# Seven feed-forward stages: one 2x2 pair of blocks of the down projection as seven products, with two of its weight sums made by adding transfers

## What is computed

```python
def swiglu(x, w_gate, w_up, w_down):
    return (jax.nn.silu(x @ w_gate) * (x @ w_up)) @ w_down

# first stack, per layer
x = x + 0.5 * swiglu(rmsnorm(x, ffn1_norm[l]), ...)
x = x + hybrid_mixer(rmsnorm(x, mix_norm[l]), ...)
x = x + 0.5 * swiglu(rmsnorm(x, ffn2_norm[l]), ...)
```

## Time and profile before

| | us |
|---|---|
| median of 3 runs (2436.86 to 2438.19) | 2436.91 |
| the profiled execution | 2436.97 |
| its span (first to last instruction) | 2435.2 |
| PE busy | 2407.2 (99%) |
| DVE busy | 1710.7 (70%) |
| ACT busy | 1255.4 (52%) |

### The profile page before, as it was taken

How to read it: one execution, slowest core, us unless ns; L and a number is a source line. 1 busy time by engine, 2 the same in 40 slices (tenths; PEclk the granted TensorE clock), 3 DMA queues, 4 the chain that set the end, 5 groups by cost and what they waited for, 6 DMA issues and landing times.

```text
span 2435.2 us, 30841 instructions
## 1 busy us (share of the span) xinstructions
PE 2407.2 (99%) x12606; PEld 2053.7 (84%) x12606; DVE 1710.7 (70%) x1755; ACT 1255.4 (52%) x1367; POOL 205.5 (8%) x358
## 2 busy tenths in 40 slices
PE   8999999999999999999999999999999999999998
PEld 6889998888889988888889878888888898778887
DVE  6555867857866778768658657777687677577884
ACT  5435545535537545445435664555455356645552
POOL 0100200101100100100100010001001000100010
PEclk9999999999999999999999999999999999999999
DMA  8765445856754446856864445468568544454672
GB/s 333 238 216 191 157 154 209 276 202 214 275 202 182 162 158 225 277 203 226 272 215 175 163 151 212 169 224 280 201 211 276 186 182 156 151 197 170 220 272 105
DMA packets 82549, 504.42 MB, mean 207 GB/s; under 512 B 11609, under 2 KB 12761, under 8 KB 30185
## 3 DMA queue, kind: packets, MB, share of 16 engines
q1 hardware_dynamic: 61488, 433.23, 49.4%
q0 software_dynamic: 19744, 67.65, 8.7%
q10 hardware_dynamic: 1176, 1.58, 0.4%
HBM read 476.72 MB, written 25.69 MB: 206 GB/s over the span
## 4 chain that ended last, share of the span: by engine, by line
PE 91%; DVE 5%; ACT 3%; issue 1%; DMA 1%; SPq 0%; POOL 0%; DVEq 0%; POOLq 0%; ACTq 0%
PE acc L709 23%; PE acc L711 22%; PE acc L710 22%; PE acc L677 4%; PE acc L678 4%; PE acc L679 4%; DVE w_lo L576 2%; PE aux L810 1%; PE aux L812 1%; PE aux L811 1%; PE aux L944 1%; ACT w_hi L568 1%; DMA raw<-in_w 1%; ACT tmp L1689 1%; PE bc L810 1%
## 5 line engine op out<-in xcount | busy, mean ns | idle before, releaser
L576 DVE TENSOR_TENSOR w_lo<-raw,w_hi 128x2048 fp32r<-128x2048 f32 (+1 forms) x438 | 978.7, 2245 | 489.1 <-ACT w_hi L568 487.9
L568 ACT ACTIVATE w_hi<-raw 128x2048 fp32r<-128x2048 f32 (+1 forms) x438 | 822.2, 1882 | 551.7 <-PE acc L711 387.6
L709 PE MATMUL acc<-w_hi,x_hi 128*128 128x512 f32 (+1 forms) x1624 | 633.4, 390 | 3.6 <-DVE x_lo L1941 2.1
L711 PE MATMUL acc<-w_lo,x_hi 128*128 128x512 f32 (+1 forms) x1624 | 628.5, 387 | 0.0
L710 PE MATMUL acc<-w_hi,x_lo 128*128 128x512 f32 (+1 forms) x1624 | 628.4, 387 | 0.0
L709 PEld LDWEIGHTS acc<-w_hi,x_hi 128*128 128x128 f32 x1624 | 305.0, 188 | 69.4 <-issue 6.1
L711 PEld LDWEIGHTS acc<-w_lo,x_hi 128*128 128x128 f32 x1624 | 305.0, 188 | 62.9
L710 PEld LDWEIGHTS acc<-w_hi,x_lo 128*128 128x128 f32 x1624 | 305.1, 188 | 61.7 <-issue 1.0
L709 PE MATMUL acc<-w_hi,h_parts 128*128 128x512 f32 x704 | 274.5, 390 | 0.0
L711 PE MATMUL acc<-w_lo,h_parts 128*128 128x512 f32 x704 | 274.0, 389 | 0.0
L710 PE MATMUL acc<-w_hi,h_parts 128*128 128x512 f32 x704 | 273.9, 389 | 0.0
(11 more groups left out here) (435 smaller groups left out, 2729.0 us busy)
## 6 DMA issues: line engine op xcount, KB each, us to landing
raw<-in_w SPq DMA_DIRECT2D x399, 1024.0 KB, 4.9
squares<-tmp POOLq DMA_DIRECT2D x40, 512.0 KB, 3.3
tmp<-squares POOLq DMA_DIRECT2D x160, 128.0 KB, 4.4
raw<-in_w SPq DMA_DIRECT2D x18, 512.0 KB, 4.8
tmp<-in_norm_gb POOLq DMA_DIRECT2D x8, 1024.0 KB, 5.9
tmp<-in_norm_gb POOLq DMA_DIRECT2D x6, 512.0 KB, 3.7
tmp<-in_gate_rows POOLq DMA_DIRECT2D x12, 256.0 KB, 2.9
squares<-tmp POOLq DMA_DIRECT2D x8, 256.0 KB, 2.8
```

The source lines that it names most:

```text
L568: nc.scalar.activation(w_hi[:, slot, 0:kind], raw[:, slots[c], 0:kind], ACT.Copy).then_inc(hi_done, 1)
L576: nc.vector.tensor_tensor(w_lo[:, slot, 0:kind], raw[:, slots[c], 0:kind], w_hi[:, slot, 0:kind].bitcast(F32), ALU.subtract).then_inc(lo_d ...
L709: nc.tensor.matmul(out, vh, wh, start=first and k == 0, stop=False)
L711: last = nc.tensor.matmul(out, vh, wl, start=False, stop=last_k and k == nk - 1)
```

## The change

In the seven FFNs behind the first, the down stage has 15 places instead of 12. The blocks of K 0 to 1023 (hid(0) and hid(1)) by both halves of the columns and both token tiles were eight block products; they are now seven, strewn among the plain chunks. The order of the places, with d = chunk 25 of the FFN and the matmuls of each:

d+0 plain, hid(2) (24); d+1 T1 (12); d+2 plain, hid(3) (24); d+3 B11 (12); d+4 B22 (12); d+5 plain, hid(4) (24); d+6 T2 (12); d+7 half, hid(5) (12); d+8 T3 (12); d+9 half, hid(5) (12); d+10 B21 (12); d+11, d+12, d+13 plain for token tile 0 (12 each); then d+11, d+12 for token tile 1 (24), d+14 T4 (12), `x_turn`, and d+13 for token tile 1 (12).

- T1 = B12 + B11: SP loads B12, and POOL then issues a transfer that adds B11 to it in `raw` (`grow`). T2 = T1 + B22 and T3 = T2 - B11 are made by DVE in `raw`. T4 = T2 + B21 is again an adding transfer, behind the last `permute`.
- The sums of hidden activations (`h_sums`, four adds of 128x512 on DVE) are made in the up stage behind `hid_low(1)`, into tmp 28 to 35 (`HQ4`); that is where the norm's gains go. They are split into `x_hi`, `x_lo` (`hsum_high`, `hsum_low`) once the up stage has used these.
- Three shared products stand in PSUM banks `bc` and `aux` and are added to `x` by six DVE instructions (`x_add`). B22, B21 and T4 go into the normal tiles.
- POOL: `load_norm` has moved from ahead of the six `permute`s to ahead of the last, behind a wait for `sum_parts` (the fourth `hsum_low`), since it overwrites the sums. The third `permute` waits for `h_sums`, and `grow` for T1 follows it.
- `add_out` of columns 0 to 511, token tile 1, has moved from the down stage into `norm`.
- A few semaphores are merged.

```diff
+DOWN = (2, D12, 3, D11, D22, 4, None, 0, None, 1, D21, 8, 9, 10, None)
+D_FIRST, D_T1, D_THREE, D_B11, D_B22, D_FOUR, D_T2, D_HALF0, D_T3, D_HALF1, D_B21, D_TWO, D_LAST2, D_LAST, D_T4 = range(15)
+DOWN_SLOT_OF = {D_FOUR: 3, D_T2: 5, D_HALF0: 3, D_T3: 5, D_B21: 3, D_TWO: 3, D_LAST2: 3, D_LAST: 3, D_T4: 8}
+DOWN_ADD = {D_T1: D11, D_T4: D21}
...
@@ PE @@
+                    plain(d + D_FIRST, 0, 8, 4, True, False)
+                    pe.wait_ge(sum_parts, 8 * b + 5)
+                    pe.wait_ge(outs_ready, 3 * b + 1)
+                    product(d + D_T1, e_, *s1, True)
+                    plain(d + D_THREE, 0, 12, 4, False, False)
+                    pe.wait_ge(kept_silu, 2 * b + 2)
+                    product(d + D_B11, b_, *h11, True)
+                    pe.wait_ge(sum_parts, 8 * b + 7)
+                    bank_free(tile + 2)
+                    into(d + D_B22, tile + 2, *s4, True, False)
+                    plain(d + D_FOUR, 0, 16, 4, False, False)
+                    pe.wait_ge(x_added, 6 * b + 3)
+                    product(d + D_T2, b_, *s2, False)
+                    plain(d + D_HALF0, 0, 20, 2, False, False)
+                    pe.wait_ge(sum_parts, 8 * b + 8)
+                    pe.wait_ge(x_added, 6 * b + 4)
+                    product(d + D_T3, b_, *s3, False)
...
+                    into(d + D_T4, tile + 1, *h22, False, True, 0)
+                    if parts(s + 1):
+                        x_turn(s + 1, 0)
+                    plain(d + D_LAST, 1, 16, 4, False, True, (1,), 2)
...
@@ ACT @@
+                    ahead.to(d + 2)
+                    hid_high(3)
+                    ended_chunk(act, d - 1)
+                    hsum_high(0)
+                    silu(5, 0)
+                    silu(5, 1)
+                    hsum_high(1)
+                    hsum_high(2)
+                    ahead.to(d + 3)
+                    hsum_high(3)
+                    choose_sqrt()
+                    ahead.to(d + 4)
+                    hid_high(4)
+                    ahead.to(d + 7)
+                    hid_high(5)
...
@@ DVE, norm @@
-                if not early:
+                if not early or s:
                     add_out(s, 0, 1)
                 add_out(s, 1, 1)
...
@@ POOL @@
+            def grow(c):
+                at = c - DOWN_AT - base[s]
+                if at == D_T1:
+                    pool.wait_ge(loaded[slots[c]], 16 * landings[c])
+                else:
+                    pool.wait_ge(lo_done, c - D_T4 + D_T2 + 1)
+                    pool.wait_ge(weight_sum, sums.index(c - D_T4 + D_T3) + 1)
+                pool.dma_start(raw[:, slots[c], 0:WIDE], t[f"w{WIDE}"][more[c]], accum_op=ALU.add).then_inc(weight_added, 16)
...
-                    load_norm(s + 1)
+                    if s == 0:
+                        load_norm(s + 1)
...
                     for i in range(6):
+                        if s and i == 2:
+                            pool.wait_ge(sum_ready, 8 * f)
+                        if s and i == 5:
+                            pool.wait_ge(sum_parts, 8 * f)
+                            load_norm(s + 1)
                         permute(f, i)
+                        if s and i == 2:
+                            grow(base[s] + DOWN_AT + D_T1)
+                    if s:
+                        grow(base[s] + DOWN_AT + D_T4)
```

More of the change, by code:

```diff
@@ L69, in transfers, with packed @@
                 place[kind] += 12
+            elif sub == "ffn" and j == DOWN_AT:
+                n = len(DOWN)
+                def packed(at):
+                    return place[WIDE] + at - (at > 5)
+                for q, at in DOWN_ADD.items():
+                    more[len(out) + q] = packed(at)
+                for q, at in enumerate(DOWN):
+                    if q in (D_HALF0, D_HALF1):
+                        out.append(place[HALF] + at)
+                    else:
+                        out.append(None if at is None else packed(at))
+                place[WIDE] += 10
+                place[HALF] += 2
             else:
@@ L73, in transfers @@
             j += n
-    return out
+    return out, more
 def wide(w):
@@ L260, in __init__ @@
                     self.block(c + last)
-                for last in (c + 24, c + 30, c + 36):
-                    self.block(last)
+                self.block(c + 24)
+                self.chunks(c + DOWN_AT + D_B21, c + DOWN_AT + D_B21 + 1)
+                self.chunks(c + DOWN_AT + D_T4, c + DOWN_AT + D_T4 + 1)
+                self.block(c + DOWN_AT + D_T4)
             if kind == "mix1":
@@ L313, in program @@
     ends = Ends(base).at
-    places = transfers()
+    places, more = transfers()
     group_at = [base[s] + GROUP_AT for s in range(n_subs) if subs[s] == "ffn"]
+    down_at = [base[s] + DOWN_AT for s in range(n_subs) if subs[s] == "ffn"]
     slots, landings, on_slot = [], [], [0] * RING
     for c, place in enumerate(places):
-        within = next((c - g for g in group_at if 0 <= c - g < len(GROUP)), 0)
-        slots.append(slots[c - SLOT_OF.get(within, RING)] if c >= RING else c)
+        back = next((SLOT_OF.get(c - g, RING) for g in group_at if 0 <= c - g < len(GROUP)), RING)
+        back = next((DOWN_SLOT_OF.get(c - d, RING) for d in down_at if 0 <= c - d < len(DOWN)), back)
+        slots.append(slots[c - back] if c >= RING else c)
         on_slot[slots[c]] += place is not None
         landings.append(on_slot[slots[c]])
-    sums = [g + q for g in group_at for q in (G_T1, G_T2, G_T3, G_T4)]
+    sums = [c for g, d in zip(group_at, down_at)
+            for c in (g + G_T1, g + G_T2, g + G_T3, g + G_T4, d + D_T2, d + D_T3)]
+    grown = sorted(more)
     with ExitStack() as ctx:
@@ L1450, in ups, with hsum_high @@
                         ahead.to(c0 + 4 * i + 7)
+                def hsum_high(q):
+                    act.wait_ge(sum_ready, 8 * (f - 1) + 4 + q + 1)
+                    nc.scalar.activation(HSUM_HI[q], HQ4[q].rearrange("p k a j -> p k (a j)"), ACT.Copy).then_inc(sum_hi, 1)
                 def group(g, b):
@@ new lines, in hsum_low, with x_add @@
+                def hsum_low(q):
+                    dve.wait_ge(sum_hi, 8 * (f - 1) + 4 + q + 1)
+                    V_.tensor_tensor(HSUM_LO[q], HQ4[q].rearrange("p k a j -> p k (a j)"), HSUM_HI[q].bitcast(F32),
+                                     ALU.subtract).then_inc(sum_parts, 1)
+                def x_add(c, bank, n, tt, sign):
+                    xs = x[:, tt, 512 * n:512 * n + 512]
+                    ended_chunk(dve, c)
+                    V_.scalar_tensor_tensor(xs, bank, sign * weight_of(s), xs, ALU.mult, ALU.add).then_inc(x_added, 1)
@@ new lines, in down @@
+                def down(d, b):
+                    b_, e_ = aux[:, 1, :], bc[:, :]
+                    ahead.to(d + 2)
+                    hid_low(3)
+                    hsum_low(0)
+                    ahead.to(d + 3)
+                    times(5, 0)
+                    times(5, 1)
+                    turn_squares(5)
+                    ahead.to(d + 4)
+                    dve.wait_ge(lo_done, d + D_T1 + 1)
+                    V_.tensor_tensor(weights(d + D_T2), weights(d + D_T1), weights(d + D_B22), ALU.add).then_inc(weight_sum, 1)
+                    hid_low(4)
+                    hsum_low(1)
+                    hsum_low(2)
+                    ahead.to(d + 5)
+                    x_add(d + D_T1, e_, 1, 0, 1.0)
+                    x_add(d + D_T1, e_, 1, 1, 1.0)
+                    ahead.to(d + 6)
+                    dve.wait_ge(weight_sum, sums.index(d + D_T2) + 1)
+                    V_.tensor_tensor(weights(d + D_T3), weights(d + D_T2), weights(d + D_B11), ALU.subtract).then_inc(weight_sum, 1)
+                    hsum_low(3)
+                    ahead.to(d + 7)
+                    x_add(d + D_B11, b_, 0, 0, 1.0)
+                    hid_low(5)
+                    ahead.to(d + 9)
+                    dve.wait_ge(x_added, 6 * b + 2)
+                    x_add(d + D_T2, b_, 1, 0, -1.0)
+                    ahead.to(d + 12)
+                    x_add(d + D_T3, b_, 0, 1, 1.0)
+                    x_add(d + D_T3, b_, 1, 1, -1.0)
+                    ahead.to(d + 13)
+                    dve.wait_ge(x_added, 6 * b + 6)
+                    add_out(s, 0, 0)
+                    ahead.to(base[s + 1] - 1)
@@ L2106, in group @@
                     hid_low(1)
+                    h_sums(b)
                     ahead.to(g + 10)
@@ L2158, in ffn @@
                 ups()
+                if s:
+                    down(c0 + DOWN_AT, f - 1)
+                    return
                 c1 = base[s + 1] - 12
```

111 lines of the change are left out of this document (87 added, 24 removed).

## The result

The changed kernel takes 2578.85 us (median of 3 runs, 2578.32 to 2580.66) against 2436.91 us: ratio 1.0582, 95% interval 1.0558 to 1.0606. It is slower by 142 us, the forecast was 93 us slower; the direction and the four places of the waits were right, the size was short by 49 us, and 2579 lies inside the range of 2475 to 2590.

What follows compares the result with a forecast made beforehand. TensorE bounds the kernel, busy 2407 of 2435 us. Terms: 7 x (1.4 + 8.0 + 3.1 + 1.0) + 6 x 2.65 + 1.4 - 19.0 = +92.8 us, forecast 2530 us, range 2475 to 2590.

Steps and rivals of the forecast that it cites:

- the four places of the waits: PE's predicted waits per down stage: before T2, before hid(5)'s first half chunk, before T3, before the next norm's second `x_turn`.
- The saving of 19.0 us: One block product of 12 matmuls fewer, 2.72 us per FFN in seven FFNs, all on the chain.
- T2's wait, 1.4 us each: PE waits before T2 for the bank that `x_add` empties: due 24.5, free 25.9, in each FFN.
- hid(5), 8.0 us each: Largest wait: POOL sends hid(5) behind the gains and `hsum_low(3)`, so it is split at 36.6, PE ready at 28.6.
- Adding transfers, 1.0 us each: T1's adding transfer stands in POOL's queue ahead of hid(3); cost taken near the low end, 1.0 us per FFN.
- My high end: Adding transfer at twice a plain 1 MB's 5.9 us, making hid(3) 5.9 us late; the low end was 0.
- the plan: The down stage laid out in us from its first matmul, T = 0, with chunks, ACT and DVE steps timed.
- T3, 3.1 us each: Before T3, PE ends the half chunk at 39.3 but `x_add` frees the bank at 42.4, behind hid(5)'s splits.
- The next norm, 2.65 us each: Behind six down stages: the next split 2.25 us later plus `add_out` 1.4 us, against 0.95 us of cover.
- the slow adding transfer: Rival, chance 0.08: adding transfer at three times a plain 1 MB, 17.7 us, ACT and DVE 9 us later; 2593 us.
- the saving is kept: Rival, chance 0.04: hid(5) lands in time if POOL is released at 14.7; 2418 us with the norm's wait gone too.
- DVE's 89%: DVE's load in the down stage: 17.7 us added to 33.9 us in 58 us, said to fit on average.

Runs made afterwards that it cites:

- experiment 3: Changed kernel with the two adding transfers per FFN made plain (part of the sums left out): 2567.95 us, ratio 1.0549.
- experiment 11: Plain transfers for the adding ones, on the changed kernel with hid(5) ahead of the gains, last products swapped, bias store in the up stage: 2492.68 us.
- Experiments 2 and 4: Each against the changed kernel: last two products swapped and `add_out` earlier, 2553.23 us; ten unused matmuls ahead of the second `x_turn`, 2572.01 us.
- Experiment 1: Changed kernel with POOL's transfer of hid(5) ahead of the wait for `sum_parts` and the gains: 2533.81 us, ratio 1.0398.
- experiment 10: T2, T3 sums cut to 64 columns, on the changed kernel with hid(5) ahead of gains, last products swapped, bias store in the up stage: 2487.72 us.

## Why the prediction was right in direction and short in size

- **The saving of 19.0 us**: right. In the sum of waits and slow matmuls of the first FFN it stands as it should: 12.3 us of pauses and 4.0 of slow matmuls less 2.72 is 13.6, and the stage grew by 13.7.
- **T2's wait, 1.4 us each**: 6.7 us over four FFNs, 1.0 in the mean, so near enough. In the other three PE had lost 2.0 to 2.3 us at B22 already and came to T2 late.
- **hid(5), 8.0 us each**: 55.0 over seven, 7.9 each, by the mechanism described. The chain of 12.5 us from the gains' issue to the split measured 12.3 (510.88 to 523.21), though its parts differ: to the first read 6.57 us behind the store's issue (5.2 to 8.0 in the seven), where store and queue were 3.75 + 1.7; the landing 2.5 us where I took 4.0. Its start was at T = 27.9 instead of 24.0, yet the wait did not grow, because PE was late at T2 by nearly as much.
- **Adding transfers, 1.0 us each**: this is the term that was mis-sized in the stage. The adding transfer lands in 8.3 us, well inside the bounds of 5.9 and 11.8, but what mattered was the queue behind it: hid(3)'s store took 9.70 us to its first read in the first FFN and 7.3 in the mean, where the same pair had 3.6 before. My high end said "delays ACT's first copy from 0.25 to about 4", and 4.2 is where it came; I took a value near the low end "since the load of T1's chunk is one of the earlier ones", and took that end for free: a plain 1 MB, "gone by then", when experiment 3 shows that even a plain one holds hid(3) up by some 2.0 us. The cost shows at B22 (2.27 us in the first FFN, a wait that I did not lay out) and in T2's start at T = 29.4 where the plan had 25.9. Experiment 3 gives 1.6 us of PE's time per FFN to the adding itself, experiment 11 2.7. What the place behind another 1 MB costs PE was not tried apart.
- **T3, 3.1 us each**: the row of the waits has only 0.7 each, but the half chunk in front of it ran 1.9 us slow behind the pause and the product began late by 1.0 us more: 2.9 in the first FFN. DVE was ready 5.6 us behind the start of the half chunk, where the plan had 5.8, so this was right; PE reached it crawling and not waiting.
- **The next norm, 2.65 us each**: 2.52 in the first FFN, so right where the norm is of that kind. In the three FFNs with the layer norm behind them PE waits 3.6 us, which I had not laid out, and all six carry 1.2 to 2.5 us more, nearly all of it slow transposes and matmuls behind the pause: 29.6 instead of 15.9 us. Experiments 2 and 4 show both parts.
- **Missing altogether**: the clock behind a pause, some 30 us in all, of which part lies in the places above (what lies between hid(5) and T3 is mostly the wait that T3 was forecast to have); B22; and the bias rows' store, to which I put down the 22 us more of the fourth FFN. I had written that the 2 MB more per FFN are hidden at a DMA share of 0.58; a mean over the stage says nothing of the one stage in which 1536 KB of small packets run beside the loads.

By its own terms: 92.8 us, and 2.2 us more in six down stages (13.1), 22.0 in the fourth, 13.7 in the norms, make 141.6. The range held it because its upper end took in the slow adding transfer; the real reasons were three smaller ones, two of which the forecast did not have, so that part is luck.

The rival *the saving is kept* named the point at which POOL would have to be released. Experiment 1 released it (hid(5) goes at T = 11.9 there) and bought 45 us of the 78 that hid(5) and T3 were to cost, since DVE's load and the adding transfers came up behind. I had found that DVE's 89% "fits on average"; experiment 10 shows that in 500 to 515 it does not.

## What to carry to other kernels

Count what a scheme adds to the engines that feed TensorE in the stretch in which it is added, not over the stage: a saved product of 2.72 us was paid with 4.6 us of weight sums on DVE, besides three more splits. Before moving a wait on an engine that issues transfers, list all that is queued behind it; here one `wait_ge` and the transfer behind it, ahead of one store, were worth 45 us. And give a pause of TensorE its full price, the pause and the slow matmuls behind it.
